# State-space layers of a decoder step: the causal mask leaves TensorE's matmuls, VectorE clamps the exponents, and the inner products are masked once per layer

## The reference

```
adt = dt * a
a_cum = cumsum(adt, axis=-1)                        # within a block of 128 tokens
cb = einsum('bcign,bcjgn->bcgij', c, b)             # inner products, one matrix per group
w = cb[:, :, :, None] * exp(segsum(adt))            # segsum: a_cum[i] - a_cum[j] for j <= i, else -inf
y_diag = einsum('bcgrij,bcjgrp->bcigrp', w, xdt)
```

## Time and profile before

| | before |
|---|---|
| median of 3 runs | 2440.27 us |
| profiled execution, its own time | 2427.95 us |
| its span, first to last instruction | 2426.2 us |
| TensorE busy | 2210.4 us (91%) |
| VectorE busy | 1234.2 us (51%) |
| ScalarE busy | 1017.1 us (42%) |
| GpSimd busy | 436.1 us (18%) |
| mean granted clock of TensorE | 0.926 |

### The profile page before, as it was taken

How to read it: one execution, slowest core, us unless ns; L and a number is a source line. 1 busy time by engine, 2 the same in 40 slices (tenths; PEclk the granted TensorE clock), 3 DMA queues, 4 the chain that set the end, 5 groups by cost and what they waited for, 6 DMA issues and landing times. The chain is left out here.

```text
span 2426.2 us, 38651 instructions
## 1 busy us (share of the span) xinstructions
PE 2210.4 (91%) x15123; PEld 1968.6 (81%) x15123; DVE 1234.2 (51%) x2108; ACT 1017.1 (42%) x1569; POOL 436.1 (18%) x428
## 2 busy tenths in 40 slices
PE   6899979999966898999977799789999999979999
PEld 4888869999965456999965466589998888879999
DVE  5666645554442234554436433255546566655554
ACT  3666654443341112443354111344434656644432
POOL 2211102441010002342000000024421111113330
PEclk9899989999985798999985599899999999989999
DMA  5244525555572442655564446156556244435654
GB/s 172 87 135 144 153 80 149 167 161 156 164 238 84 115 135 80 174 158 155 158 189 143 160 158 212 35 148 174 155 159 186 79 144 144 138 105 164 168 148 139
DMA packets 505226, 352.45 MB, mean 145 GB/s; under 512 B 13547, under 2 KB 486397, under 8 KB 504217
## 3 DMA queue, kind: packets, MB, share of 16 engines
q1 hardware_dynamic: 503906, 323.01, 45.7%
q0 software_dynamic: 1152, 27.13, 3.4%
HBM read 326.59 MB, written 50.63 MB: 155 GB/s over the span
## 5 line engine op out<-in xcount | busy, mean ns | idle before, releaser
L249 PE MATMUL ps<-xh,wh 128*128 128x288 f32 x2368 | 652.8, 303 | 16.3 <-ACT wh L213 16.2
L249 PE MATMUL ps<-xl,wh 128*128 128x288 f32 x2368 | 643.8, 298 | 0.0
L221 DVE TENSOR_TENSOR wl<-raw,wh 128x2048 fp32r<-128x2048 f32 (+3 forms) x241 | 501.3, 2082 | 242.0 <-ACT wh L213 242.0
L213 ACT ACTIVATE wh<-raw 128x2048 fp32r<-128x2048 f32 (+3 forms) x241 | 418.6, 1740 | 269.1 <-PE ps L257 229.7
L249 PEld LDWEIGHTS ps<-xh,wh 128*128 128x128 f32 x2368 | 452.7, 191 | 18.3 <-issue 14.2
L249 PEld LDWEIGHTS ps<-xl,wh 128*128 128x128 f32 x2368 | 452.3, 191 | 0.5
L257 PE MATMUL ps<-xh,wl 128*128 128x288 f32 x2368 | 353.3, 300 | 0.0
L257 PEld LDWEIGHTS ps<-xh,wl 128*128 128x128 f32 x2368 | 326.9, 190 | 2.3
L472 POOL TENSOR_TENSOR gh<-sg,ut 128x288 f32<-128x288 f32 x88 | 216.7, 2463 | 351.5 <-ACT sg L411 351.5
L249 PE MATMUL ps<-hh,wh 128*128 128x288 f32 x704 | 191.0, 296 | 0.0
L249 PE MATMUL ps<-hl,wh 128*128 128x288 f32 x704 | 190.9, 297 | 0.0
(11 more groups left out here) (318 smaller groups left out, 3112.6 us busy)
## 6 DMA issues: line engine op xcount, KB each, us to landing
raw<-in_ffn_w_in SPq DMA_DIRECT2D x176, 512.0 KB, 5.1
raw<-in_ssm_w_in SPq DMA_DIRECT2D x80, 512.0 KB, 4.8
raw<-in_ffn_w_out SPq DMA_DIRECT2D x64, 384.0 KB, 4.2
raw<-in_ffn_w_out SPq DMA_DIRECT2D x64, 320.0 KB, 3.4
H<-in_state_ssm SPq DMA_DIRECT2D x32, 512.0 KB, 7.4
out_ssm_sample<-H SPq DMA_DIRECT2D x32, 512.0 KB, 6.3
raw<-in_ssm_w_out SPq DMA_DIRECT2D x32, 512.0 KB, 5.3
Kp<-in_cache_diff_k SPq DMA_DIRECT2D x64, 256.0 KB, 4.1
```

Of the source, the lines that this page charges most:

```text
L213: act.activation(wts["hi"][:, s, 0:width], raw[:, s, 0:width], ACT.Copy).then_inc(hi_ready.sem, 1)
L221: dve.tensor_tensor(wts["lo"][:, s, 0:width], raw[:, s, 0:width], wts["hi"][:, s, 0:width].bitcast(F32), ALU.subtract).then_inc(lo_ready.s ...
L249: pe.matmul(out, W[0][:, kk, j, :], x_[:, k, :], stop=False, start=(part == 0 and kk == 0 and x_ is seg.hi), skip_group_check=True)
```

## The change

- `spread(h)` is one matmul; the mask matmul (L1043) is gone.
- VectorE gets `clamp(h)`: three instructions, one for each token tile, which read bank 6, add the column of `nack` and take the minimum with 0, and write E. They wait for the spread, for ea_ready of the chunk, and for E's buffer. On VectorE `clamp(2k)` stands ahead of `update(k-1, 0)` and `clamp(2k+1)` behind `more_taps`.
- `decay(h)` on ScalarE is one exponential of E in place over all 288 columns, and waits for the clamps.
- `move_cb` moves from ScalarE to VectorE and multiplies by the mask (tri, tris) as it moves the inner products, once per layer.
- TensorE's waits for E (e_ready) ahead of the next spread and of `sum_squares` become waits for the clamps.

```diff
                 def spread(h):
                     c = h // 2
-                    pe.wait_ge(e_ready.sem, e_ready.at(3 * h))
+                    pe.wait_ge(clamped.sem, clamped.at(3 * h))
...
-                    pe.matmul(out, id2[:, h:h + 1].to_broadcast([2 * HEADS, P]), acHL[:, :], start=True, stop=False,
-                              skip_group_check=True)
-                    pe.matmul(out, idr[:, :], after[:, :], start=False, stop=True, skip_group_check=True).then_inc(
-                        ac_spread.sem, ac_spread.inc())
+                    pe.matmul(out, id2[:, h:h + 1].to_broadcast([2 * HEADS, P]), acHL[:, :], start=True, stop=True,
+                              skip_group_check=True).then_inc(ac_spread.sem, ac_spread.inc())
...
                 def decay(h):
-                    if h == 0:
-                        act.wait_ge(nac_ready.sem, nac_ready.at(1))
-                    act.wait_ge(ac_spread.sem, ac_spread.at(h + 1))
-                    if h >= 4:
-                        act.wait_ge(y_mm.sem, y_mm.at(h - 3))
-                    for t in range(3):
-                        act.activation(E[:, h % 4, cols_of(t)], ps[:, 6, cols_of(t)], ACT.Exp,
-                                       bias=nack[:, t, h:h + 1]).then_inc(e_ready.sem, e_ready.inc())
+                    act.wait_ge(clamped.sem, clamped.at(3 * h + 3))
+                    act.activation(E[:, h % 4, :], E[:, h % 4, :], ACT.Exp).then_inc(e_ready.sem, e_ready.inc())
...
+                def move_cb():
+                    dve.wait_ge(zeroed.sem, zeroed.at(3))
+                    for g in range(GROUPS):
+                        bank = 7 - 3 * (g % 2)
+                        dve.wait_ge(cb_mm.sem, cb_mm.at(g + 1))
+                        dve.tensor_tensor(
+                            cb[:, g, 0:SEQ].rearrange("p (t n) -> p t n", t=2),
+                            ps[:, bank, 0:SEQ].rearrange("p (t n) -> p t n", t=2),
+                            tri.unsqueeze(1).to_broadcast([P, 2, P]), ALU.mult).then_inc(cb_ready.sem, cb_ready.inc())
+                        dve.tensor_tensor(cb[0:NS, g, SEQ:TOK], ps[0:NS, bank, SEQ:TOK], tris[0:NS, 0:NS],
+                                          ALU.mult).then_inc(cb_ready.sem, cb_ready.inc())
+
+                def clamp(h):
+                    dve.wait_ge(ac_spread.sem, ac_spread.at(h + 1))
+                    dve.wait_ge(ea_ready.sem, ea_ready.at(h // 2 + 1))
+                    if h >= 4:
+                        dve.wait_ge(y_mm.sem, y_mm.at(h - 3))
+                    for t in range(3):
+                        dve.tensor_scalar(E[:, h % 4, cols_of(t)], ps[:, 6, cols_of(t)], nack[:, t, h:h + 1], 0.0,
+                                          ALU.add, ALU.min).then_inc(clamped.sem, clamped.inc())
...
+                    clamp(2 * k)
                     if k >= 1:
                         update(k - 1, 0)
                     if what == "x":
                         more_taps(n)
+                    clamp(2 * k + 1)
+                    if k == 0:
+                        move_cb()
```

More of the change, by code:

```diff
@@ L833, in ssd @@
                      "tail_moved"))
-            chunk_rows, bs_hi, bs_lo, us_hi, us_lo = (
-                S(n) for n in ("chunk_rows", "b_sample_hi", "b_sample_lo", "u_hi", "u_lo"))
+            clamped, chunk_rows, bs_hi, bs_lo, us_hi, us_lo = (
+                S(n) for n in ("decay_clamped", "chunk_rows", "b_sample_hi", "b_sample_lo", "u_hi", "u_lo"))
             strow_in, stored = S("strow_in", 16), S("stored", 16)
@@ L1187, in _ @@
                         g = k // 4 - 1
-                        pe.wait_ge(e_ready.sem, e_ready.at(6 * k + 6))
+                        pe.wait_ge(clamped.sem, clamped.at(6 * k + 6))
                         sum_squares(g, range(4 * g, 4 * g + 4))
@@ L1200, in _ @@
                 y_across(CI - 1)
-                pe.wait_ge(e_ready.sem, e_ready.at(3 * HEADS))
+                pe.wait_ge(clamped.sem, clamped.at(3 * HEADS))
                 pe.wait_ge(ea_ready.sem, ea_ready.at(CI))
@@ L1237, in weigh @@
                 def weigh(h):
-                    pool.wait_ge(e_ready.sem, e_ready.at(3 * h + 3))
+                    pool.wait_ge(e_ready.sem, e_ready.at(h + 1))
                     pool.wait_ge(cb_ready.sem, cb_ready.at(2 * GROUPS))
@@ L1322, in split_b @@
                         act.activation(BtS[q * NS:(q + 1) * NS, :], Bs[:, :], ACT.Copy).then_inc(bs_hi.sem, bs_hi.inc())
[L1324 to L1331, removed]
                 def split_u(c):
@@ L1438, in _ @@
                     move_state(k, 1)
-                    if k == 0:
-                        move_cb()
                 move_tail(0)
@@ L1689, in build_program @@
     kv_rows = lambda ap, b: ap[0, b].rearrange("w k h d -> w (k h d)")
-    qkv_moved = S("qkv_moved")
     def qkv_evac(dst):
```

## The result

The changed kernel takes 2480.98 us (median of four runs, 2469.61 to 2482.98); its ratio to the kernel before is 1.0154, 95% interval 1.0116 to 1.0193. It is slower by 1.5%. The forecast was 2437 us, no measurable change, with 2424 to 2458 as range. The profiled execution has a span of 2477.8 us, 51.6 over that of before; the granted clock of TensorE fell from 0.926 to 0.907. (The medians are 41 us apart: the profiled execution of before was 12 us under its median, that of the changed kernel 1.5 us.)

A forecast was written before the change was run, and what follows sets the result against it. TensorE was taken to bound the kernel. Savings and new waits summed to -2.4 us a layer, -4.8 for both, with 1.5 for the clock -3.3: from the median 2440.27 to 2437 us, range 2424 to 2458.

The forecast's parts named there:

- masks and the chunk spread's restart: TensorE, chunk loop: 0.33 us per mask matmul and 0.20 for the restart were to save 0.86 us a step.
- TensorE's stalls: Ahead of sums_of_chunk behind steps with taps: TensorE idle 1.15 us, about 2.3 us in steps 7 and 11.
- granted clock: TensorE's clock in the loop: no fall summed; only 1.5 us added for half clock in layer 3's step 0.
- The clamps: VectorE, three operations a head reading PSUM: 0.65 us summed, 0.6 to 0.8 possible; at 0.8 the total is 2441 us.
- The chain: Steps with taps: clamp(2k) through taps, clamp(2k+1) and exponential to move_state ends at +9.76 us; TensorE is there at +8.65.
- step 15 and the end of the layer: Step 15, at half clock: two masks of about 0.5 us and the chunk spread's restart saved, -1.4 us a layer.
- the fall of the clock behind the new stalls: Slower rival: half clock after stalls in the loop, 3 us a fall, 2455 us at six falls; chance 0.25 with longer chain.
- The second layer's step 0: Products start 1.2 us later; TensorE idles some 3 us more, so 1.5 us added for half clock, between nothing and 3.
- The faster rival: Steps with taps: the chain doesn't reach TensorE, each gives 0.86 us, total 2417 us; chance 0.10 wholly, 0.15 in part.

The follow-up runs named there:

- the mask experiment: Kernel before with the mask matmul taken out and nothing in its place (result not the reference's): 2405.77 us, ratio 0.9854 to the kernel before.
- ScalarE's other order: Changed kernel with silu, squares and move_state(k,1) ahead of the exponential of head 2k+1 in steps with taps: 2417.3 us, ratio 0.9932 to the kernel before.
- run 17: Not a run number: the run with ScalarE's other order, from the changed kernel, was 17 us under the kernel before beside it; 2417.3 us, ratio 0.9932.
- the mask kept: Changed kernel with the mask matmul put back into spread, clamps and moved work staying: 2504.03 us, ratio 1.0253 to the kernel before.
- the kernel before stalled: Kernel before with two needless squares ahead of each square on ScalarE, so move_state(k,1) comes late: 2488.38 us, ratio 1.0184 to the kernel before.

## Why the prediction was wrong

For one of the two loops, with the counting of the windows above (step 1's chunk spread to step 15's):

| term | forecast, us | measured, us |
|---|---|---|
| masks and the chunk spread's restart | 14 x -0.86 = -12 | -12.2 (mask alone gone) |
| TensorE's stalls | 0.5 + 4 x 1.15 + 2 x 2.35 = +9.8 | +11.6 (second layer 12.2) |
| granted clock | 0 | +21.1 (second layer 19.9): the rest of +20.5 and +19.9; some 18 to 20 of it is the clock |

The rest is not all clock. Matmuls overlap by 0.16 us, so a stall of 1.36 us sets TensorE back by 1.52; that is 1.1 us for the seven of a loop. Against the step lengths of the mask experiment, the falls themselves come to some 38 us in the two loops together.

- **What bounds the kernel, what a mask matmul costs:** right. Reading its cost from the distance to the next matmul, 0.33 us, and not from columns or duration gave 13.65 us a step, and 13.66 was measured. That two 64-row matmuls would stand 0.13 us apart was wrong (0.24); another term made up for it.
- **The clamps:** three took 0.77 us with the next operation 0.68 behind their start; 0.65 was summed, 0.8 the upper bound. **move_cb** on VectorE was hidden: the 24 products of step 0 of the first layer took 5.67 us, as before:

```profile
101.03 5.67 PE L1016 MATMUL ps<-BC 128*128 128x128 f32 x24 [2.96 <-ACT BC L1274]
```

- **The chain:** right in its links, a little short in length: in step 3 move_state ended 10.04 us after the even spread (145.55 to 155.59), where 9.76 was summed. In step 3 TensorE stood still for 1.36 us (forecast 1.15), in step 7 for 2.56 (2.35), in step 1 for 0.74 (0.5). Steps without a stall were 13.65 us long. Step 9 had 1.26 us (1.78 in the second layer), step 13 1.77: there VectorE was still at the gates when the decays were ready, so the clamp came later. Step 0 of the first layer became 1.1 us longer, 1.2 was summed; the idle time ahead of its products grew by 2.1 us. Of step 15 and the end of the layer (first spread to the next projection's first matmul), 1.1 us went in the first layer, where 1.4 was summed; in the second 2.1 us came, with more time at half the clock.
- **The step that failed:** the forecast put the fall of the clock behind the new stalls as a rival, in a class with 0.25, and left it at zero in the sum, with +1.5 us in step 0 alone. Its reason was that the clock had not fallen in steps 1 to 14 of the kernel before, though the four-column matmuls stood there. That said nothing of four-column matmuls behind a stall, and a stall was what the same forecast brought into every second step. The row that did speak of it was step 15: idle time beside those matmuls, then half the clock. In the changed kernel the clock fell behind 13 of the 14 stalls (not behind step 9 of the first layer), and once more without one. A short fall made the step 1.6 us longer; in steps 8 and 12 the fall lasted 10 to 14 us and cost 4.5 to 6.2. The rival had the mechanism and, at 3 us a fall, about the price (38 us for fourteen is 2.7); what it had wrong was the number: six falls gave 2455, fourteen came.
- **The second layer's step 0:** +5.7 us, where the sum had 1.2 and 1.5 for the clock, at most 3. Its clock stayed at half for all of these 17 us, where the kernel before had 0.90 (second row, from 3 us earlier in the step); its 24 products took 5.67 us instead of 3.35:

```profile
1920.00:1937.00 17.00, 13.28 (x54) 11.45 (x55) 6.88 (x22) 6.39 (x10) 3.23 (x3) 0.50 0.00 0
1894.00:1911.00 17.00, 12.46 (x84) 10.95 (x82) 5.94 (x14) 13.08 (x32) 4.31 (x6) 0.90 0.08 27
```

- **The faster rival** (the chain doesn't reach TensorE) is what ScalarE's other order makes of the change, though the forecast 2417 and the measured 2417.3 agree by luck: the rival was 23 us under the kernel before, the run 17.

That the clock is the cause rests on three runs: filler that only adds work takes 25 us back, taking the stalls away takes 54 back (0.0222 of 2434) where their own length is 24, and stalls of 13 us put into the kernel before cost 45. What stays open is when a stall makes the clock fall: 0.74 us did in both layers of the changed kernel, 1.10 us in two cases of eight with the clamp ahead of the taps, 0.39 in neither layer with the mask kept, 0.44 in both with the clamp ahead. In all the clock fell behind 13 of 14 stalls in the changed kernel, 11 of 14 with the mask kept, 6 of 14 with the clamp ahead, 6 of 12 in the kernel before stalled, each counted in one execution. Length and the matmuls around it don't settle that; the place in time may play a part; that is not shown, no run here isolates it.

## What to carry to other kernels

Work moved from the bounding engine to an idle one is free in busy time, but follow it in the queue: whatever stands behind the new instruction, on its engine and on the next one, moves back by all that stands ahead of it, here by the taps. When the forecast finds a new stall of TensorE in a loop that used to run without one, price it by more than its length: give the matmuls behind it at half the clock a term of its own in the sum, and a range wide enough for a fall behind half of the stalls or behind all. And before giving such a change up, look whether the late link can be taken out of the chain: here it was an exponential that nobody needed before the next step.

## What the runs showed of the hardware

- A stall of 1.05 us in each second 14.5 us step, ahead of some 3 us of small matmuls (250.97 to 254.3 in the kernel before stalled), took the granted clock of the loop from 1.00 to 0.93 and 0.88 in a kernel whose loop had run at full speed. A short fall cost 1.6 us in the changed kernel; five here lasted 17 us and cost 7.5 each.
- Between a 64-row and a 128-row matmul of 288 columns 0.32 to 0.33 us pass, whichever comes first; two 64-row matmuls stand 0.24 us apart with 288 columns in the first, two streaming 128-row ones 0.13. The 96-row one comes 0.16 us behind a 64-row one of 160 columns, but 0.27 where a 128-row one stood ahead of the pair; why is open. The Trainium skill, TensorEngine Tiling (Array Packing), Key Properties, has the drain at a change of mode; these rows agree for 64 against 128 rows.
- Needless matmuls in a stall can make a kernel faster: 25 us here, against the changed kernel.
